# The last stage's second accumulator: added in SBUF by its own transfer from GpSimd instead of by VectorE, with six output tiles in flight instead of four

## What is computed

```python
x = x + merged @ w_o                                   # after the mixer
h2 = rmsnorm(x, g_ffn).reshape(b * s, d)
shared = swiglu(h2, s_gate, s_up, s_down)
routed = routed_experts(h2, w_router, router_bias, e_gate, e_up, e_down)
x = x + (shared + routed).reshape(b, s, d)
return rmsnorm(x, g_final)
# swiglu(h, g, u, d) = (silu(h @ g) * (h @ u)) @ d
```

## Time and profile before

| | |
|---|---|
| median of 3 runs | 2683.92 us (2683.74 to 2684.55) |
| the profiled execution's own time | 2684.11 us |
| its span, first to last instruction | 2682.4 us |
| last stage, from SP's first tile load to the end | 2554.98 to 2682.4 us |
| busy in the span: PE, DVE, ACT, POOL | 97%, 67%, 46%, 49% |

### The profile page before, as it was taken

The page is one execution under the profiler, slowest core; times in us unless marked ns, Lnnn a source line. Parts: engine busy times, 40 slices in busy tenths (PEclk is TensorE's granted clock), DMA queues, the critical chain, the costliest instruction groups (busy, mean ns, idle before and its releaser), DMA issues.

```text
span 2682.4 us, 50981 instructions
## 1 busy us (share of the span) xinstructions
PE 2605.6 (97%) x11854; PEld 2150.5 (80%) x11855; DVE 1793.2 (67%) x2536; ACT 1230.8 (46%) x1742; POOL 1313.8 (49%) x1094
## 2 busy tenths in 40 slices
PE   7999999999999999939999999999999999999998
PEld 6888888888888888827888888888888888888886
DVE  5544555656555656657877877777877777777677
ACT  3223323232323233216666666566666666666532
POOL 3000002120122013367877887777877877777722
PEclk9999999999999999959999999999999999999999
DMA  8233423442343334438988988888988888888676
GB/s 320 94 101 103 145 97 101 128 156 94 102 133 133 118 103 124 144 123 241 291 241 267 296 269 243 240 245 250 287 260 247 265 229 245 235 239 253 185 246 213
DMA packets 170062, 523.52 MB, mean 195 GB/s; under 512 B 37738, under 2 KB 43548, under 8 KB 170016
## 3 DMA queue, kind: packets, MB, share of 16 engines
q1 hardware_dynamic: 96224, 345.46, 35.8%
q0 software_dynamic: 65584, 163.32, 25.7%
q10 hardware_dynamic: 8208, 14.16, 1.6%
HBM read 434.94 MB, written 119.18 MB: 207 GB/s over the span
## 4 chain that ended last, share of the span: by engine, by line
PE 54%; POOL 0%; DVE 0%; DMA 0%; issue 0%; DVEq 0%; ACT 0%; POOLq 0%
PE ps_gu L1561 12%; PE ps_gu L1559 12%; PE ps_gu L1560 12%; PE ps_y L1561 6%; PE ps_y L1560 6%; PE ps_y L1559 6%; PE ps_h L1615 1%; POOL xs L1488 0%; DMA xs<-h_dram,gidx 0%; DVE xt L1773 0%; POOL rstd L1537 0%; DVEq L1793 0%; DVE y L1868 0%; DVE xl L1784 0%; DVE expert_raw L1858 0%
## 5 line engine op out<-in xcount | busy, mean ns | idle before, releaser
L1488 POOL DMA_INDIRECT xs<-h_dram,gidx x656 | 821.3, 1252 | 201.7 <-issue 198.7
L1559 PE MATMUL ps_gu<-expert_hi,xl 128*128 (+1 forms) x1392 | 542.8, 390 | 21.4 <-DVE xl L1784 18.8
L1768 DVE TENSOR_TENSOR expert_lo<-expert_raw,expert_hi 128x1024 f32 (+1 forms) x390 | 459.6, 1220 | 129.6 <-ACT expert_hi L1645 129.3
L1561 PE MATMUL ps_gu<-expert_hi,xh 128*128 (+1 forms) x1392 | 543.2, 390 | 0.0
L1560 PE MATMUL ps_gu<-expert_lo,xh 128*128 (+1 forms) x1392 | 542.6, 390 | 0.0
L967 DVE TENSOR_TENSOR ul<-raw,uh 128x1024 fp32r<-128x1024 f32 x185 | 226.6, 1225 | 404.7 <-ACT uh L785 400.6
L1645 ACT ACTIVATE expert_hi<-expert_raw 128x1024 f32 (+1 forms) x390 | 390.9, 1052 | 70.8 <-issue 36.1
L95 POOL TENSOR_SCALAR rstd<-mean 128x1 f32<-128x1 f32 x29 | 7.4, 254 | 847.2 <-ACT junk L804 846.9
L544 PE MATMUL ps_t<-hh,ul 128*128 128x512 f32 x1024 | 402.0, 393 | 3.8 <-DVE hl L1193 3.8
L545 PE MATMUL ps_t<-hl,uh 128*128 128x512 f32 x1024 | 399.6, 390 | 0.0
L546 PE MATMUL ps_t<-hh,uh 128*128 128x512 f32 x1024 | 399.4, 390 | 0.0
(11 more groups left out here) (291 smaller groups left out, 3920.5 us busy)
## 6 DMA issues: line engine op xcount, KB each, us to landing
expert_raw<-experts SPq DMA_DIRECT2D x396, 512.0 KB, 5.8
raw<-units SPq DMA_DIRECT2D x190, 512.0 KB, 3.3
xs<-h_dram,gidx POOLq DMA_INDIRECT x656
h_dram<-h ACTq DMA_DIRECT2D x17, 512.0 KB, 4.7
acc_odd<-h POOLq DMA_DIRECT2D x17, 512.0 KB, 15.7
acc<-x SPq DMA_DIRECT2D x4, 2048.0 KB, 8.2
expert_raw<-acc_odd SPq DMA_DIRECT2D x16, 512.0 KB, 6.4
expert_raw<-x POOLq DMA_DIRECT2D x14, 512.0 KB, 3.7
```

The costliest lines, as they stand in the source:

```text
L1488: nc.gpsimd.indirect_dma_start(xs[s][:, g * DQ:(g + 1) * DQ], None, h2_quarters, bass.IndirectOffsetOnAxis(ap=gidx[s][:, g:g + 1], axis=0) ...
L1559: nc.tensor.matmul(out_, sl, vh, start=first, stop=False)
L1561: return nc.tensor.matmul(out_, sh, vh, start=False, stop=last)
L1768: V.tensor_tensor(l_, raw[:, p, :], h_, ALU.subtract).then_inc(piece_ready, 1)
```

## The change

TILES goes from 4 to 6, and the six `tile_acc` buffers are the two `y` and four slices of `raw`; `tile_odd` is gone. SP loads `acc` alone. For `acc_odd`, POOL waits until tile t of `acc` has landed and issues a transfer from `acc_odd` straight onto `tile_acc`, with the addition done by the transfer (`accum_op=ALU.add`); its semaphore is `tile_sum`. POOL issues the first six of these before its first `tile_root`, and the one of tile t + 4 behind the store of tile t. On DVE, `sum_tile` and the drain are gone, and `add_shared` and `add_half` wait for `tile_sum`.

```diff
-TILES = 4
+TILES = 6
...
-        tile_acc = [y[0], y[1], raw[:, 0, :], raw[:, 1, :]]
-        tile_odd = [raw[:, 2 + k, :] for k in range(TILES)]
+        tile_acc = [y[0], y[1]] + [raw[:, k, :] for k in range(TILES - 2)]
...
                 sp.dma_start(tile_acc[k][:, :], acc_tiles[0][t]).then_inc(tile_in[k], 16)
-                sp.dma_start(tile_odd[k], acc_tiles[1][t]).then_inc(tile_in[k], 16)
...
+            def add_odd(t):
+
+                k = t % TILES
+                pool.wait_ge(tile_in[k], (t // TILES + 1) * 16)
+                carry(pool, marks)
+                pool.dma_start(tile_acc[k][:, :], acc_tiles[1][t], accum_op=ALU.add).then_inc(tile_sum[k], 16)
+
             pool.drain()
+            for t in range(TILES):
+                add_odd(t)
             for t in range(NT - 2):
                 tile_root(t)
                 store(t)
+                if TILES <= t + 4 < NT:
+                    add_odd(t + 4)
...
-            def sum_tile(t):
-
-                k = t % TILES
-                dve.wait_ge(tile_in[k], (t // TILES + 1) * 32)
-                V.tensor_tensor(tile_acc[k][:, :], tile_acc[k][:, :], tile_odd[k], ALU.add)
-
             def add_shared(t):
 
                 s, k = t % 2, t % TILES
-                dve.drain()
+                dve.wait_ge(tile_sum[k], (t // TILES + 1) * 16)
                 dve.wait_ge(down_done, n * 2 + (t + 2))
...
             hidden_low(n * 2 + (NT - 1), (NT - 1) % 2)
-            sum_tile(NT - 1)
             add_eps(NT - 3)
             add_shared(NT - 2)
```

More of the change, by code:

```diff
@@ L1406, in mixture @@
         tile_in = [sem(f"tile_in{k}") for k in range(TILES)]
+        tile_sum = [sem(f"tile_sum{k}") for k in range(TILES)]
         tile_out = [sem(f"tile_out{k}") for k in range(TILES)]
@@ L1856, in add_half @@
                 acc_half = tile_acc[t % TILES][:, half]
+                dve.wait_ge(tile_sum[t % TILES], (t // TILES + 1) * 16)
                 dve.wait_ge(down_done, n * 2 + (t + 2 + h))
@@ L1883, in _ @@
                         x_turn(n * 2 + (t + 3), (t + 3) % 2, (t + 3 - AHEAD) // 2 * 64 + 64, rows_in)
[L1884 to L1887, removed]
                 if t >= 2:
@@ L1891, in _ @@
                     scale(t - 3)
-                if t == LATE:
-                    sum_tile(t - 1)
                 if LATE <= t < NT - 1:
```

## The result

The kernel got slower: 2690.90 us, the median of 12 runs (2690.06 to 2693.21), against 2684.52 (2683.29 to 2688.26) of the kernel before, in 12 runs, the three of the table above among them. The ratio is 1.0019, with a 95% interval of 1.0011 to 1.0027, which is 5.1 us (2.9 to 7.2) of 2684.5; the two medians, 6.4 us apart, agree with that. The forecast of 2682.3 us was wrong, and its range to 2685.4 didn't hold the time.

A forecast was written before the change was run, and what follows sets the result against it. PE was taken to bound the stage, except at its two ends. 2684.11 - 2.7 (end) + 1.1 (stall at the start) = 2682.5 us, less 0.2 to the runs' median: 2682.3; own range 2681.5 to 2683.9, whole range up to 2685.4.

The forecast's parts named there:

- The bound and the place: Last stage: PE sets the pace, 8.4 us per tile; only the stage's start and end decide the time.
- The end: End of last stage: without `sum_tile(15)`, `add_half` starts earlier, a gain of 2.7 us, at most 2.9.
- The middle: Tiles 0 to 13: removed additions gain nothing, DVE idles some 2.4 us per round, DMA engines just full at 8.0 to 8.4.
- The start: Start of last stage: tile 0's second transfer follows the first, `add_shared(0)` starts at 2566.3, PE stalls 1.1 us.
- third term: Tile 0's adding transfer: its eight packets per engine wait for eight others from SP's queue, 1.3 us.
- the step from the landing of `acc` to POOL's issue: Tile 0 at the start: POOL wakes and issues the adding transfer 0.66 us after `acc` lands, at 2559.24.
- The longer stall: Rival, chance 0.17: first adding transfer lands later than 2567.8, stall exceeds the 2.7 us gain, up to 4.7; 2685.9 us.
- No stall: Rival, chance 0.22: at the start the adding transfer lands within 6 us, leaving the gain alone; 2681.2 us.
- no gain at the end: Rival, chance 0.06: tile 15's sum is late or another wait replaces the transfer's; 2685.0 us.
- transfers as the bound: Rival, chance 0.05: adding takes 5.8 us or more per tile, DMA engines fall behind in the middle; at 7 us, 2693.

The follow-up runs named there:

- the last sum left out: Kernel before without `sum_tile(15)`, so tile 15 lacks `acc_odd` and `add_half` waits for its loads instead; ratio 0.9995 [0.9985, 1.0004], stage 124.7 us.
- both queues held: Changed kernel, SP's loads from tile 2 and ACT's round 2 rows held until tile 0's transfer is done: adding, ratio 1.0010; plain, one run, stage 130.3 us.
- SP's loads held: Changed kernel, but SP waits until tile 0 is summed before loading tile 2 and later; ratio 0.9996 [0.9987, 1.0005], stage 125.5 us.
- The long wait in the kernel before: Kernel before with seven DVE additions into a tile that nothing reads, ahead of `hidden_low(2)`; ratio 1.0022 [1.0012, 1.0031], stage 134.5 us.
- the kernel with tiles 0 and 1 on DVE: Changed kernel, but SP loads both accumulators of tiles 0 and 1 and DVE adds them, POOL from tile 2; 2683.41 us, ratio 0.9989.
- The kernel with the plain transfer and loaded queues: Changed kernel with tile 0's `acc_odd` transfer plain, so tile 0 lacks `acc`, all queues loaded as in the change; one run, stage 128.4 us.

## Why the prediction was wrong

**The bound and the place: right.** PE sets the pace and only the two ends decide. PE's one wait is at the place I named, behind `hidden_low(2)`; it is `turn_hidden(3)`, whose start at 2570.42 stands just ahead of `down(2)` at 2570.55, so there were 3.84 us of slack in place of 3.97.

**The end: right.** 2.7 us were predicted; the changed kernel got 2.6, and the last sum left out 2.7.

**The middle: right.** The DMA engines are at 1.00 ("just full"), PE doesn't wait for them, and DVE's timeline has 2.46 us of idle time at a round's start, predicted "near 2.4":

```profile
2606.07 0.42 DVE L1802 TENSOR_TENSOR hid<-ps_gu,sg 128x256 f32<-128x256 f32 x1 [2.46 <-ACT sg L1679]
```

**The start: the step that failed.** The prediction's three terms for the first adding transfer were 4.1 for a plain one, 1.6 for the adding and 1.3 for "eight others of a plain transfer", 7.0 in all. Measured they are 3.7, 1.8 and 4.1, 9.6 in all. The third term failed, by 2.8 us. I took it from the earlier trace rows, where SP's and ACT's queues, both long under way, share packet for packet, and carried that over to a transfer that is issued behind a full queue. The packets by queue show otherwise. In the changed kernel from 2563 to 2567, with POOL's transfer issued at 2562.71, its queue q0 has no line at all (packets, MB, share of 16 engines):

```profile
q1 hardware_dynamic: 320, 1.18, 81.8%
q10 hardware_dynamic: 135, 0.13, 11.7%
```

With both queues held it has packets from 2563 on, within 2 us of its issue at 2561.62, and no company to 2567:

```profile
q0 software_dynamic: 175, 0.65, 100.0%
```

This is not POOL's queue alone. ACT's row loads in the changed kernel, issued at 2560.74, have no packet from 2561 to 2564 either. And the trace of the kernel before had the same place to read: ACT's issue there on the timeline, and the one line of the packets by queue from 2559 to 2561.9, which is SP's.

```profile
2558.05 2.82 ACTq L1738 DMA_DIRECT2D xs<-h_dram  x4
...
q1 hardware_dynamic: 257, 0.95, 97.2%
```

With SP's loads held, ACT's rows were issued at 2561.51 and had 61 packets between 2562 and 2563 already. So the third term was to be read at the stage's start, where a transfer waits some 4 us behind SP's loads, and not from a window well inside it.

The page "DMA: Bandwidth & Descriptors" of the Trainium skill, section "Queues, rings and completion order", says that each DMA engine takes turns between the queues that have work, a packet at a time. By that POOL's transfer would have had its share from the start, as I assumed; the trace agrees for SP's and ACT's queues well inside the stage and disagrees at its start, for POOL's queue and for ACT's, unless their packets come to the engines so much later than the issue. Which of the two it is, no run here settles.

A second miss in the same chain is the step from the landing of `acc` to POOL's issue. I took 0.66 us from a store that waits for DVE. From the landing (2557.53 + 3.3 = 2560.83) to the issue at 2562.71 it was 1.88 us, 1.2 more. It was not the hand-over that took longer. For tile 2 POOL did wait for the landing, and there it was 0.54 us from 2558.39 + 6.3 = 2564.69 to the issue (its load with us to landing, and POOL's timeline):

```profile
expert_raw<-acc SPq DMA_DIRECT2D x1, 512.0 KB, 6.3
...
2565.23 0.88 POOL L1550 DMA_DIRECT2D expert_raw<-acc_odd  x1 [0.58 <-DMA expert_raw<-acc]
```

At tile 0 POOL itself was late. The chain of work that ended last has these pieces there: POOL's drain ahead of the adding transfers (line 1552), a stretch in which POOL waits for nothing that the profile shows ("issue"), and the mark that POOL sets once it has seen tile 0's landing (line 86):

```profile
2553.15 1.73 POOLq L1552
2554.88 7.26 issue
2562.14 0.02 POOLq L86
```

The timeline puts POOL's idle time of 7.84 us down to the landing, but that lay 1.3 us back when POOL set the mark. The 7.26 us are the same in all seven kernels in which POOL issues tile 0's transfer, whatever their loads; what POOL does in them no view shows. `acc` itself landed 0.3 sooner than taken. In sum `add_shared(0)` came 14.83 us after SP's first load, predicted 11.3 (2566.3 - 2554.98), and the stall was 4.6 in place of 1.1 us: both 3.5 more, which is 2.6 + 1.2 - 0.3.

**What had no term.** The clock. A wait was priced at its own length; in the changed kernel it cost 4.6 us and then 2.4 more at a granted clock of 0.50. The long wait in the kernel before shows that by itself. By the prediction's sum the stage would have taken 127.4 - 2.7 + 1.1 = 125.8 us; it took 132.1. Of the 6.3 us between them 3.5 are the stall, 2.4 the clock and 0.1 the smaller gain; the 0.3 left over lie ahead of `turn_hidden(3)`, within the 15.4 to 15.7 us by which the profiles differ there.

**The rivals.** The longer stall came true, to which I gave 0.17. Its price for the stall, up to 4.7 us, held; without the clock its time of 2685.9 was too low. No stall, no gain at the end and transfers as the bound are out: the first by the wait, the second by the 2.6 us, the third by the kernel with tiles 0 and 1 on DVE, which has the same DMA share and no loss. The kernel with the plain transfer and loaded queues is close to the rival as I had priced it: a wait of 3.2 us, a clock of 1.00, and a stage of 128.4.

**Still open** is why a transfer issued at the stage's start gets its first packets only behind the others' work, and what decides on the clock besides the length of a wait: it stayed at 1.00 behind waits of 2.6 and 3.2 us, and fell behind waits of 2.2 and 3.1 us in the two kernels with both queues held, where PE had waited once before. What fills POOL's 7.26 us ahead of its first issue is open too.

## What to carry to other kernels

A transfer that is issued behind a full set of others is priced by what those queues still have to move, and not by its own bytes alone: ask where its first packet will stand, above all at the start of a stage, where all loads are issued at once. Replace the steady state by the new way and leave the first one or two tiles to the old, where both ways exist: here that kept the gain and took away the loss. And where PE is the bound, the price of one stall includes the stretch at the lower clock behind it, which here was 2.4 us on top of 4.6.

## What the runs showed of the hardware that I had not expected

- A 512 KB transfer from POOL, issued some 5 us after SP began to issue six loads of the same size, was ready 8.3 us (plain) and 9.6 us (adding) after its issue, and 3.7 and 5.5 us with nothing else under way. For comparison, the fit in the Trainium skill that the prediction cited, "DMA: Bandwidth & Descriptors", section "Anatomy of one DMA", makes it 3.2 us; the trace agrees roughly for the plain transfer on free queues alone.
- An adding transfer took POOL 0.87 to 0.93 us to issue in the changed kernel (the first two together 1.93), a plain store 0.58 to 0.62; the prediction had taken them for the same.
- A transfer that waited some 4 us or more for its first packet behind SP's loads was not only POOL's: ACT's row loads had the same at the same place, in the kernel before as well (issued at 2558.05, no packet from 2559 to 2561.9).
- PE's granted clock was 0.50 for some 5 us behind one wait of 4.6 us, in a stage in which it had been busy without a gap, and the same fall came from a wait made by DVE's additions alone.
